# Three products of a two-block layer, each as seven chained products of halves

## The chip, the cores and the metric

One NeuronCore of one Trainium2 chip runs the whole program. The metric is the device time of one execution in microseconds. Three executions of the kernel before took 1607.38, 1607.43 and 1607.52 us.

## The reference, cut to what matters

The program computes two transformer-like blocks over 512 tokens of 1024 features in float32. The part that changes is the middle of the second block:

```
att  = forgetting_attention(q, k, v)            # 512 x 1024
mix  = gmlp_spatial_gating(z_u, z_v)            # 512 x 1024
ga, gb = sigmoid(gate columns)                  # 512 x 1024 each
h = x + (ga * (mix @ w_branch_a) + gb * (att @ w_branch_b)) @ w_out
h = h + ffn(rmsnorm(h))                         # starts with the product "up0"
```

Each of the three products is 512x1024 by 1024x1024.

## The kernel before, in words

**Precision.** A float32 product is made of three passes. Each operand is split into a high part (`fp32r`, by a ScalarE copy) and a low part (raw minus high, by a VectorE subtraction), and TensorE adds high x high, high x low and low x high in PSUM (`feature_k`).

**Weights.** All weights come as strips of 128x2048 floats (1 MB), 4 to a 1024x1024 matrix, through three slots (`w_raw`, which lies in the place of `w_lo`, and `w_hi`). The SyncE queue loads a strip as soon as the one three places back has been used; `hi(s)` on ScalarE and `lo(s)` on VectorE split it. Every engine works through an order of instructions that is written out by hand, and the engines meet in counting semaphores: `unit_done` (TensorE's half strips), `hi_split`, `strip_split`, `dve_evac` and others.

**The three products.** `stream("branch_b")`, `stream("branch_a")` and `stream("out2")` (lines 1277 to 1279) each run 8 output tiles of 128 features x 512 tokens, 24 matmuls of 512 columns each: 192 matmuls a product. The activations are `att_t` (split into `b_hi`, `b_lo` during the product before, `gate_a`), `u_t` (split into `a_hi`, `a_lo`) and `merged` (split tile by tile as it comes out). VectorE takes each tile out of PSUM as it multiplies by the gate, adds to `merged`, or adds to `x`. After `out2` tile m has been added to `x`, `high("ffn2")` and `low("ffn2")` split it for `up0`, the next product. GpSimd does nothing in this stretch. (Line 2116 adds a PSUM bank to `att_t` in SBUF.)

**Elsewhere** two kinds of products are already made of seven products of halves (`seven`, line 1172). There the sums of weight halves come from GpSimd's DMA queue: a transfer from DRAM that adds into a strip already in SBUF (`part_sums`, line 714). Each such transfer waits until the one before has landed.

Of the kernel before, what the change touches and what calls it, by code (L numbers as in the profile page):

```python
# [162 lines left out]
def build(nc, d, out):  # L163
    ctx = ExitStack()
    with ctx:
# [139 lines left out]

        up_pad = [sb(f"up_pad{j}", [P, CONV2 - 1 + T], at=work + 2048 + 520 * j) for j in range(4)]
# [104 lines left out]
        m_hi = sem("m_hi")  # L411
        m_lo = sem("m_lo")
# [10 lines left out]
        amix_hi = sem("amix_hi")  # L423
        amix_lo = sem("amix_lo")
# [32 lines left out]
        pool_out_ready, POOL_OUT0 = seg_done, SPARE0 + 32 * len(SEVEN)  # L457

# [73 lines left out]
        def _(sp_eng):  # L532
# [49 lines left out]

            for s in range(1, N_STRIPS):
# [6 lines left out]
                sp_eng.dma_start(w_raw[j].rearrange("p k n -> p (k n)"), d["strips"][STRIP_AT[s]]).then_inc(raw_loaded[j], 16)  # L590
# [4 lines left out]
                if s + 1 in MADE:  # L595
                    other_parts(SEVEN.index(next(name for name in SEVEN if FIRST[name] == s + 1)))
# [29 lines left out]
        def _(pool):  # L626
# [100 lines left out]
            attention("2b", "qk2b")  # L727
            for g in range(FF_SEVEN, len(SEVEN)):
# [9 lines left out]
        def _(pe):  # L738
# [630 lines left out]
        def _(act):  # L1369
# [416 lines left out]
            def sigmoids(phase, where):  # L1786
                for j in range(KT):
# [20 lines left out]
            for i in range(2, 4):
                hi(FIRST["branch_b"] + i + 2)
            for m in range(KT):  # L1810
                act.wait_ge(merged_ready, m + 1)
                if m == 0:

                    act.wait_ge(unit_done, 2 * FIRST["branch_a"])
                run(b_hi[:, m, :], merged[:, m * T:(m + 1) * T], ACT.Copy).then_inc(m_hi, 1)
                if m % 2 == 0:
                    hi(FIRST["branch_a"] + m // 2 + 2)
            for m in range(KT):
                act.wait_ge(dve_evac, EVAC0["out2"] + m + 1)
# [125 lines left out]
        def _(dve):  # L1945
# [959 lines left out]
```

## Time and profile before

| | us |
|---|---|
| median of three executions | 1607.43 |
| the profiled execution | 1607.59 |
| its span, first to last instruction | 1605.9 |
| TensorE busy in the span | 1587.6 (99%) |
| VectorE busy | 1078.5 (67%) |
| ScalarE busy | 710.6 (44%) |
| GpSimd busy | 181.5 (11%) |

Matmuls are pipelined, so their durations overlap: the pace is the distance between starts. An engine's row in order of time gives the start from the span's start, and the duration. "idle before <-" names what ended an idle time.

### The profile page before, as it was taken

To read this page: it belongs to the slowest core of one execution; us is meant where nothing else is said; L and a number is where in the kernel's file an instruction comes from. 1 tells how busy PE (TensorE), PEld (TensorE's weight loads), DVE (VectorE), ACT (ScalarE), POOL (GpSimd) and SP (SyncE) were. 2 spreads that over 40 slices of the span, in tenths; PEclk is the share of its full clock that TensorE was granted. 3 is DMA by queue.
4 is the path that set the end of the run, shared out by engine and by line. 5 is a ranking of instruction groups with operands and counts; after the bars stand their busy time and mean duration, and the time that the engine had idled before them with its cause. 6 is when DMAs were issued, how large, how long until landed. Compare 5 with 4: busy or idle time off the path is not lost.

```text
span 1605.9 us, 20446 instructions
## 1 busy us (share of the span) xinstructions
PE 1587.6 (99%) x8187; PEld 1305.8 (81%) x8187; DVE 1078.5 (67%) x1494; ACT 710.6 (44%) x1018; POOL 181.5 (11%) x263
## 2 busy tenths in 40 slices
PE   9999999999999999999999999999999999999998
PEld 7877777888888888878788887888888888888888
DVE  6756788669393865657744477445566876878857
ACT  6524575545252524415662156342334443443544
POOL 0001055000000000024500255000000000000000
PEclk9999999999999999999999999999999999999999
DMA  5233321264757522331022211322237347344221
GB/s 191 80 106 125 123 95 53 79 210 131 236 132 235 131 106 94 116 138 72 27 105 83 101 53 53 136 101 105 93 143 262 102 135 238 93 154 158 105 106 53
DMA packets 32894, 195.14 MB, mean 122 GB/s; under 512 B 4320, under 2 KB 6816, under 8 KB 11296
## 3 DMA queue, kind: packets, MB, share of 16 engines
q1 hardware_dynamic: 25056, 160.20, 27.0%
q0 software_dynamic: 2880, 20.97, 6.8%
q10 hardware_dynamic: 4864, 12.66, 2.2%
q8 instruction: 65, 1.06, 0.3%
q14 instruction: 29, 0.24, 0.0%
HBM read 187.50 MB, written 6.32 MB: 121 GB/s over the span
## 4 chain that ended last, share of the span: by engine, by line
PE 87%; DVE 7%; issue 2%; ACT 2%; POOL 1%; DMA 0%; DVEq 0%; ACTq 0%; POOLq 0%
PE bank L767 20%; PE bank L769 19%; PE bank L768 19%; PE bank L1189 3%; PE bank L1190 3%; PE bank L1191 3%; PE bank L815 3%; PE bank L817 3%; PE bank L816 3%; PE bank L1000 1%; PE bank L775 1%; PE bank L985 1%; DVE w_lo L2370 1%; PE bank L744 1%; DVE up_c L2668 1%
## 5 line engine op out<-in xcount | busy, mean ns | idle before, releaser
L767 PE MATMUL bank<-a_hi,w_hi 128*128 128x512 f32 x1160 | 456.8, 394 | 0.6 <-DVE x L2030 0.6
L769 PE MATMUL bank<-a_hi,w_lo 128*128 128x512 f32 x1160 | 452.0, 390 | 0.0
L768 PE MATMUL bank<-a_lo,w_hi 128*128 128x512 f32 x1160 | 451.6, 389 | 0.0
L1375 ACT ACTIVATE w_hi<-w_raw 128x2048 fp32r<-128x2048 f32 x95 | 181.3, 1908 | 184.5 <-DMA w_raw<-in_strips 182.7
L769 PEld LDWEIGHTS bank<-a_hi,w_lo 128*128 128x128 f32 x1160 | 217.8, 188 | 45.9
L767 PEld LDWEIGHTS bank<-a_hi,w_hi 128*128 128x128 f32 x1160 | 217.9, 188 | 45.3 <-issue 2.3
L768 PEld LDWEIGHTS bank<-a_lo,w_hi 128*128 128x128 f32 x1160 | 218.0, 188 | 43.0 <-issue 0.2
L1951 DVE TENSOR_TENSOR w_lo<-w_raw,w_hi 128x2048 fp32r<-128x2048 f32 x92 | 210.9, 2293 | 54.4 <-ACT w_hi L1375 54.3
L1189 PE MATMUL bank<-w_hi,t_hi 128*128 128x512 f32 x280 | 109.3, 390 | 0.1
L1191 PE MATMUL bank<-w_hi,t_lo 128*128 128x512 f32 x280 | 109.0, 389 | 0.0
L1190 PE MATMUL bank<-w_lo,t_hi 128*128 128x512 f32 x280 | 109.0, 389 | 0.0
L767 PE MATMUL bank<-b_hi,w_hi 128*128 128x512 f32 x240 | 93.6, 390 | 0.4 <-DVE b_lo L2684 0.4
L768 PE MATMUL bank<-b_lo,w_hi 128*128 128x512 f32 x240 | 93.4, 389 | 0.0
L769 PE MATMUL bank<-b_hi,w_lo 128*128 128x512 f32 x240 | 93.4, 389 | 0.0
L815 PE MATMUL bank<-w_hi,a_hi 128*128 128x512 f32 x224 | 90.8, 405 | 0.0
L714 POOL DMA_DIRECT2D a_part<-in_parts x20 | 17.4, 868 | 643.6 <-DMA a_part<-in_parts 431.9
L816 PE MATMUL bank<-w_lo,a_hi 128*128 128x512 f32 x224 | 87.4, 390 | 0.0
L817 PE MATMUL bank<-w_hi,a_lo 128*128 128x512 f32 x224 | 87.4, 390 | 0.0
L1845 ACT ACTIVATE up_c<-up_pad,conv_w 128x512 f32<-128x512 f32 x44 | 35.8, 816 | 115.1 <-DVE up_pad L2022 115.1
L2668 DVE SCALAR_TENSOR_TENSOR up_c<-up_pad,conv_w,up_c 128x512 f32<-128x512 f32 x88 | 65.8, 747 | 1.8 <-ACT up_c L1845 0.3
L2370 DVE TENSOR_TENSOR w_lo<-a_part,w_hi 128x2048 fp32r<-128x2048 f32 x25 | 57.1, 2285 | 10.7 <-ACT w_hi L1664 10.7
L2022 DVE TENSOR_TENSOR up_pad<-bank,rstd 128x512 f32<-128x512 f32 x44 | 30.3, 691 | 49.4 <-PE bank L769 49.4
(364 smaller groups left out, 2658.0 us busy)
## 6 DMA issues: line engine op xcount, KB each, us to landing
w_raw<-in_strips SPq DMA_DIRECT2D x107, 1024.0 KB, 4.8
a_part<-in_parts SPq DMA_DIRECT2D x25, 1024.0 KB, 7.4
a_part<-in_parts POOLq DMA_DIRECT2D x20, 1024.0 KB, 9.1
spare<-in_parts SPq DMA_DIRECT2D x5, 1024.0 KB, 15.0
spare<-in_strips SPq DMA_DIRECT2D x5, 1024.0 KB, 4.9
seg_in<-cum_kept ACTq DMA_DIRECT2D x16, 256.0 KB, 3.5
x_kept<-x ACTq DMA_DIRECT2D x2, 2048.0 KB, 9.2
x<-x_kept SPq DMA_DIRECT2D x2, 2048.0 KB, 9.9
```

The source lines that it names most:

```text
L767: mm(ps[:, :], w_hi[slot][:, k, cols], hi[:, k, :], start=(k == 0), stop=False)
L768: mm(ps[:, :], w_hi[slot][:, k, cols], lo[:, k, :], start=False, stop=False)
L769: return mm(ps[:, :], w_lo[slot][:, k, cols], hi[:, k, :], start=False, stop=(k == kt - 1))
L815: mm(bank[j][:, :], hi[:, q, tok], w_hi4[slot][:, k, :], start=(q == 0), stop=False)
L816: mm(bank[j][:, :], hi[:, q, tok], w_lo4[slot][:, k, :], start=False, stop=False)
L817: return mm(bank[j][:, :], lo[:, q, tok], w_hi4[slot][:, k, :], start=False, stop=(q == KT - 1))
L1189: mm(ps[:, :], hi[:, k, tok], w_hi4[slot][:, k, :], start=(first and k == 0), stop=False)
L1190: mm(ps[:, :], hi[:, k, tok], w_lo4[slot][:, k, :], start=False, stop=False)
L1191: last = mm(ps[:, :], lo[:, k, tok], w_hi4[slot][:, k, :], start=False, stop=(end and k == W4 - 1))
L1375: run(w_hi[j], w_raw[j], ACT.Copy).then_inc(hi_split, 1)
L1951: v.tensor_tensor(w_lo[j], w_raw[j], w_hi[j].bitcast(F32), ALU.subtract).then_inc(strip_split, 1)
L2668: v.scalar_tensor_tensor(up_c[q], up_pad[q][:, j:j + T], flat[:, at * (CONV2 + 1) + j:at * (CONV2 + 1) + j + 1], up_c[q], ALU.mult, ALU.ad ...
```

## The change

Each of the three products is cut into halves: the activation into four quadrants (256 tokens x 512 input features), the weight into four parts (512 x 512, one strip each), and the result is put together from seven products of a quadrant-sized activation by a part-sized weight, with sums and differences of quadrants and of parts as operands. One product is 4 output tiles x 4 input tiles x 3 passes = 48 matmuls of 256 columns; seven make 336.

- **Weights.** Of the seven weight operands two are parts as they are (products 2 and 6, loaded by SyncE into a slot). Two (products 0 and 4) are made in a buffer `fold_v`, and three (1, 3 and 5) in a buffer `fold_u`. In each buffer a first part is loaded by SyncE (`load_v`, `load_u`), and further parts are added by GpSimd's DMA (`add_part`), one add before products 1, 3, 4 and 5. An add changes the buffer in place, so it comes after the operand before it in that buffer has been split. All adds wait for the landing of the add before them, in the order of `FOLD_SUMS`. `fold_u` and `fold_v` of `branch_b` and `branch_a` are the same place; `out2` has its own, over `att_t`.
- **Low parts.** ScalarE still makes all high parts. VectorE makes the low parts of products 1, 2, 3, 5 and 6 (`low_strip`), GpSimd those of 0 and 4 (`low_v`, 128x2048).
- **Activations.** GpSimd makes four sums or differences of quadrants a product (`fold_sums`, 128x1024 each). Seven quadrant operands are split by ScalarE (`high_four`, `high_three`) and VectorE (`low_four`, `low_three`).
- **Results.** Products 0 and 2 are chained in banks 4 and 5, products 1 and 3 in 6 and 7, products 4 and 6 in 2 and 3; product 5 goes to 6 and 7. ScalarE copies the first link of two chains out before the next is added (`keep_first`, `keep_second`), VectorE takes out the rest (`take_first`, `keep_sums`, `take`) and multiplies or adds quadrants; for `out2` it adds known parts to `x` ahead of time (`add_known`).
- **Reload of x** moves from the end of `gate_a` to `branch_a`'s product 6, since `fold_v` and `fold_u` lie in `x`.
- **Before up0** VectorE's order is: `take_21`, the low part of `up0`'s first strip, feature tiles 0 to 3 of the split for `up0`, `take_12`, the second strip, tiles 4 to 7.

The diff, cut, with 12 leading spaces taken off:

```diff
+FOLD = ["branch_b", "branch_a", "out2"]
+QUADS = [(0, 0), (1, 0), (0, 1), (1, 1)]
+FOLD_BANK = [4, 6, 4, 6, 2, 6, 2]
+FOLD_QUAD = [0, 1, 2, 0, 1, 3, 2]
+FOLD_DIRECT = {2: (1, 0), 6: (1, 1)}
+V_STEPS, U_STEPS = [0, 4], [1, 3, 5]
+FOLD_ADD = {1: (1, 1), 3: (0, 0), 4: (0, 1), 5: (1, 0)}
+FOLD_SUMS = [(0, 1), (0, 4), (0, 3), (0, 5), (1, 1), (1, 4), (1, 3), (2, 1), (1, 5), (2, 4), (2, 3), (2, 5)]
+PHASES += [(name, 7) for name in FOLD]
...
+def load_v(f):
+    if f == 1:
+        sp_eng.wait_ge(pool_split, pool_count(0, 4))
+    sp_eng.dma_start(flat(fold_v[f]), fold_part(f, (0, 0))).then_inc(v_loaded, 16)
+def load_u(f):
+    if f == 1:
+        sp_eng.wait_ge(strip_split, FIRST[FOLD[0]] + 6)
+    sp_eng.dma_start(flat(fold_u[f]), fold_part(f, (0, 1))).then_inc(u_loaded, 16)
...
-    if s == FIRST["gate_a"] + 3:
+    if s == FIRST["gate_a"] + 2:
         sp_eng.wait_ge(pv_done, 2 * 3 * HEADS8)
+        load_v(0)
+        load_u(0)
+    if s == FIRST["branch_b"] + 2:
+        load_v(1)
+    if s == FIRST["branch_b"] + 6:
+        load_u(1)
+    if s == FIRST["branch_a"] + 2:
+        sp_eng.wait_ge(fold_step, FOLD_STEP0 + 5)
+        load_v(2)
+        load_u(2)
+    if s == FIRST["branch_a"] + 6:
+        sp_eng.wait_ge(strip_split, FIRST["branch_a"] + 6)
+        sp_eng.wait_ge(pool_split, pool_count(1, 4))
         sp_eng.dma_start(x, x_kept).then_inc(x_loaded[0], 16)
...
+def add_part(f, i):
+    if i == 1:
+        pool.wait_ge(u_loaded, U_LOADED0 + 16 * (f + 1))
+    elif i == 4:
+        pool.wait_ge(pool_split, pool_count(f, 0))
+    else:
+        pool.wait_ge(strip_split, FIRST[FOLD[f]] + i - 1)
+    landed, count = fold_count(f, i)
+    pool.wait_ge(landed, count - 16)
+    pool.dma_start(flat(fold_raw(f, i)), fold_part(f, FOLD_ADD[i]), accum_op=ALU.add).then_inc(summed, 16)
+def low_v(f, i):
+    s = FIRST[FOLD[f]] + i
+    pool.wait_ge(hi_split, s)
+    pool.tensor_tensor(w_lo[s % W_SLOTS], fold_v[f], w_hi[s % W_SLOTS].bitcast(F32), ALU.subtract).then_inc(pool_split, 1)
+def fold_sums(f, n):
+    src, at = fold_src[f], FOLD_SUM0 + 4 * f
+    a11, a12, a21, a22 = (quad(src, *q) for q in ((0, 0), (0, 1), (1, 0), (1, 1)))
+    if n == 0:
...
+        ins = pool.tensor_tensor(quad(fold_three[f], 1, 0), a11, a21, ALU.subtract)
+    elif n == 1:
+        pool.wait_ge(fold_sum, at + 1)
+        ins = pool.tensor_tensor(a21, a21, a22, ALU.subtract)
...
+    elif n == 2:
+        pool.wait_ge(fold_sum, at + 2)
+        pool.wait_ge(four_lo, 4 * f + 1)
+        ins = pool.tensor_tensor(a11, a21, a11, ALU.subtract)
+    else:
+        pool.wait_ge(fold_sum, at + 3)
+        pool.wait_ge(four_lo, 4 * f + 3)
+        ins = pool.tensor_tensor(a12, a12, a11, ALU.add)
+    ins.then_inc(fold_sum, 1)
+fold_sums(0, 0)
+add_part(0, 1)
+fold_sums(0, 1)
+fold_sums(0, 2)
+low_v(0, 0)
+add_part(0, 4)
+fold_sums(0, 3)
+add_part(0, 3)
+fold_sums(1, 0)
+fold_sums(1, 1)
+add_part(0, 5)
+low_v(0, 4)
+fold_sums(1, 2)
+fold_sums(1, 3)
+add_part(1, 1)
+low_v(1, 0)
+add_part(1, 4)
+add_part(1, 3)
+add_part(2, 1)
+add_part(1, 5)
+low_v(1, 4)
+low_v(2, 0)
+add_part(2, 4)
+fold_sums(2, 0)
+fold_sums(2, 1)
+add_part(2, 3)
+fold_sums(2, 2)
+fold_sums(2, 3)
+add_part(2, 5)
+low_v(2, 4)
...
+def folded(f):
+    for i in range(7):
+        s = FIRST[FOLD[f]] + i
+        slot, (t, k0) = s % W_SLOTS, QUADS[FOLD_QUAD[i]]
+        hi, lo = quad(fold_hi[f], t, k0), quad(fold_lo[f], t, k0)
+        if i in V_STEPS:
+            pe.wait_ge(pool_split, pool_count(f, i))
+        else:
+            pe.wait_ge(strip_split, s + 1)
+        if i in (3, 4, 6):
+            pe.wait_ge(three_lo, 3 * f + (3, 4, 6).index(i) + 1)
+        else:
+            pe.wait_ge(four_lo, 4 * f + (0, 1, 2, 5).index(i) + 1)
+        for h in range(2):
+            fold_bank(f, i, h)
+            for e in range(2):
+                ps = bank[FOLD_BANK[i] + h][:, e * (T // 2):(e + 1) * (T // 2)]
+                cols = slice((2 * h + e) * P, (2 * h + e + 1) * P)
+                for k in range(W4):
+                    mm(ps, w_hi4[slot][:, k, cols], hi[:, k, :], start=(e == 0 and k == 0 and i in (0, 1, 4)), stop=False, skip_group_check=True)
+                    mm(ps, w_hi4[slot][:, k, cols], lo[:, k, :], start=False, stop=False, skip_group_check=True)
+                    last = mm(ps, w_lo4[slot][:, k, cols], hi[:, k, :], start=False, stop=(k == W4 - 1), skip_group_check=True)
+            last.then_inc(unit_done, 1)
...
+def high_three(f, n):
+    t, k = QUADS[n]
+    act.wait_ge(fold_sum, FOLD_SUM0 + 4 * f + (3, 2, 4)[n])
+    act.wait_ge(unit_done, 2 * (FIRST[FOLD[f]] + n) + 2)
+    run(quad(fold_hi[f], t, k), quad(fold_src[f], t, k), ACT.Copy).then_inc(three_hi, 1)
...
+def keep_first(f):
+    act.wait_ge(four_lo, 4 * f + 4)
+    act.wait_ge(fold_sum, FOLD_SUM0 + 4 * f + 2)
+    for h in range(2):
+        act.wait_ge(unit_done, 2 * FIRST[FOLD[f]] + h + 1)
+        run(quad(fold_src[f], 1, 1, h), halves(4 + h), ACT.Copy).then_inc(snapped, 1)
...
+def low_strip(f, i):
+    s = FIRST[FOLD[f]] + i
+    j = s % W_SLOTS
+    dve.wait_ge(hi_split, s)
+    v.tensor_tensor(w_lo[j], fold_raw(f, i), w_hi[j].bitcast(F32), ALU.subtract).then_inc(strip_split, 2 if i - 1 in V_STEPS else 1)
...
+def keep_sums(f):
+    src, e0 = fold_src[f], EVAC0[FOLD[f]]
+    for h in range(2):
+        product_ready(f, 3, h)
+        dve.wait_ge(snapped, SNAPPED0 + 4 * f + h + 1)
+        v.tensor_tensor(quad(src, 0, 0, h), halves(6 + h), quad(src, 1, 1, h), ALU.add).then_inc(dve_evac, 1)
+    for h in range(2):
+        dve.wait_ge(dve_evac, e0 + 2 + h + 1)
+        dve.wait_ge(snapped, SNAPPED0 + 4 * f + 2 + h + 1)
+        fold_do(v.tensor_tensor(fold_q[h], quad(src, 0, 0, h), fold_q[h], ALU.subtract))
+def take(f, i, j, step, at):
+    src, e0 = fold_src[f], EVAC0[FOLD[f]]
+    for h in range(2):
+        product_ready(f, step, h)
+        known = {(1, 1): quad(src, 0, 0, h), (1, 0): quad(src, 1, 1, h), (0, 1): fold_q[h]}[i, j]
+        if f == 2:
+            part = quad(x, i, j, h)
+            ins = v.tensor_tensor(part, part, halves(FOLD_BANK[step] + h), ALU.add)
+        else:
+            ins = v.tensor_tensor(quad(src, 1, 0, h), halves(FOLD_BANK[step] + h), known, ALU.add if (i, j) == (1, 0) else ALU.subtract)
+        ins.then_inc(dve_evac, 1)
+    if f == 2:
+        return
+    dve.wait_ge(dve_evac, e0 + at + 2)
+    new, gate, total = quad(src, 1, 0), quad(gate3, i, j), quad(merged3, i, j)
+    if f == 0:
+        fold_do(v.tensor_tensor(total, total, new, ALU.mult))
...
+low_four(1, 0)
+low_strip(0, 2)
+low_three(0, 0)
+low_four(1, 1)
+low_strip(0, 3)
+low_three(0, 1)
+take_first(0)
+low_four(1, 2)
+low_three(0, 2)
+keep_sums(0)
+low_strip(0, 5)
+low_four(1, 3)
+take_22(0)
+low_strip(0, 6)
+take_21(0)
+low_strip(1, 1)
+take_12(0)
+low_strip(1, 2)
+low_three(1, 0)
+low_strip(1, 3)
+low_three(1, 1)
+take_first(1)
+low_three(1, 2)
+low_four(2, 0)
+keep_sums(1)
+low_strip(1, 5)
+take_22(1)
+low_strip(1, 6)
+take_21(1)
+low_strip(2, 1)
+take_12(1)
+low_four(2, 1)
+low_four(2, 2)
+low_four(2, 3)
```

ScalarE's order for one product is: high of product 2's weight, `keep_first`, `high_three` 0, `high_four` 1 of the next, high of 3, `keep_second`, `high_three` 1, high of 4, and so on to the next product's strips 0 and 1; `high_strip(f, 1)` stands ahead of `high_strip(f, 2)`.

## Rows read from the trace of the kernel before

**Rows 1.** The page: busy time by engine; the chain that ended last.
```profile
PE 1587.6 (99%) x8187; PEld 1305.8 (81%) x8187; DVE 1078.5 (67%) x1494; ACT 710.6 (44%) x1018; POOL 181.5 (11%) x263
...
PE 87%; DVE 7%; issue 2%; ACT 2%; POOL 1%; DMA 0%; DVEq 0%; ACTq 0%; POOLq 0%
```

**Rows 2.** Stretches: busy PE, PEld, DVE, ACT, POOL; PEclk; DMA share; GB/s.
```profile
1057.00:1101.00 44.00, 44.00 (x196) 36.44 (x195) 19.04 (x20) 10.36 (x10) 0.00 (x0) 1.00 0.26 97
1101.00:1145.00 44.00, 44.00 (x196) 36.44 (x195) 25.21 (x28) 12.28 (x12) 0.00 (x0) 1.00 0.27 96
1145.00:1188.00 43.00, 43.00 (x192) 35.59 (x191) 24.17 (x28) 17.79 (x22) 0.00 (x0) 1.00 0.28 98
```

**Rows 3.** TensorE in time: start us, duration us; 575 matmuls between.
```profile
1052.45 0.39 PE L767 MATMUL bank<-b_hi,w_hi 128*128 128x512 f32 x1
...
1183.01 0.39 PE L767 MATMUL bank<-a_hi,w_hi 128*128 128x512 f32 x1
```

**Rows 4.** TensorE in time, last stage; 95 matmuls between.
```profile
1571.76 0.28 PE L1325 MATMUL bank<-a_hi,w_hi 128*128 128x256 f32 x1
...
1583.28 0.28 PE L1325 MATMUL bank<-a_hi,w_hi 128*128 128x256 f32 x1
```

**Rows 5.** Groups by form, VectorE, ScalarE: busy us, mean ns | idle before.
```profile
L1951 DVE TENSOR_TENSOR w_lo<-w_raw,w_hi 128x2048 fp32r<-128x2048 f32 x92 | 210.9, 2293 | 54.4 <-ACT w_hi L1375 54.3
...
L2392 DVE TENSOR_TENSOR t_lo<-t_raw,t_hi 128x1024 fp32r<-128x1024 f32 x25 | 30.4, 1216 | 0.0
...
L1986 DVE SCALAR_TENSOR_TENSOR a_lo<-x,gains,a_hi 128x512 fp32r<-128x512 f32 x32 | 23.9, 750 | 25.0 <-ACT a_hi L1396 25.0
...
L2626 DVE TENSOR_TENSOR merged<-merged,bank 128x512 f32<-128x512 f32 x8 | 5.5, 686 | 24.5 <-PE bank L769 24.5
...
L1375 ACT ACTIVATE w_hi<-w_raw 128x2048 fp32r<-128x2048 f32 x95 | 181.3, 1908 | 184.5 <-DMA w_raw<-in_strips 182.7 <-issue 1.7
...
L1676 ACT ACTIVATE t_hi<-t_raw 128x1024 fp32r<-128x1024 f32 x25 | 26.5, 1059 | 39.3 <-DVE t_raw L2386 39.3
...
L1899 ACT ACTIVATE ple_t<-bank 128x512 f32<-128x512 f32 x8 | 4.1, 604 | 4.0 <-PE bank L1302 4.0
```

**Rows 6.** Groups by form, GpSimd.
```profile
L734 POOL TENSOR_TENSOR out_t<-x,rstd 128x256 f32<-128x256 f32 x2 | 1.4, 723 | 188.3 <-ACT rstd L1935 188.3
...
L674 POOL TENSOR_SCALAR score<-score,row_inv 128x512 f32<-128x512 f32 x8 | 5.6, 695 | 8.8 <-DVE row_inv L2105 8.6
...
L2896 POOL MEMSET const-float32-1.0<- 128x1 f32 x1 | 0.1, 98 | 0.0
```

**Rows 7.** VectorE and GpSimd in time, at two places.
```profile
710.11 2.28 DVE L1951 TENSOR_TENSOR w_lo<-w_raw,w_hi 128x2048 fp32r<-128x2048 f32 x1
...
710.28 2.58 POOL L667 TENSOR_SCALAR q_blk<-qk 64x512 fp32r<-64x512 f32 x1 [48.33 <-DVE qk L2022]
...
909.47 2.69 DVE L1951 TENSOR_TENSOR w_lo<-w_raw,w_hi 128x2048 fp32r<-128x2048 f32 x1
...
909.09 3.55 POOL L667 TENSOR_SCALAR k_blk<-qk 64x512 fp32r<-64x512 f32 x2
```

**Rows 8.** Line 2116: duration ns min/median/max.
```profile
L2116 DVE TENSOR_TENSOR att_t<-att_t,bank x16: 678/686/692, 754.6 to 1010.0; 64x512 f32<-64x512 f32 x16
```

**Rows 9.** DMA issues (KB, median us to landing); line 714; GpSimd in time.
```profile
w_raw<-in_strips SPq DMA_DIRECT2D x107, 1024.0 KB, 4.8
...
a_part<-in_parts SPq DMA_DIRECT2D x25, 1024.0 KB, 7.4
...
a_part<-in_parts POOLq DMA_DIRECT2D x20, 1024.0 KB, 9.1
...
DMA to landing us min/median/max: 7.6/9.1/13.1
...
1222.26 0.87 POOL L714 DMA_DIRECT2D a_part<-in_parts  x1 [8.18 <-DMA a_part<-in_parts]
```

**Rows 10.** TensorE in time, the first matmuls.
```profile
1.39 7.46 PE L1051 MATMUL bank<-b_lo 128*128 128x512 f32 x19 [1.39 <-POOL b_lo L628]
```

More of the change, by code:

```diff
@@ L1282, in _ @@
+            for f in range(len(FOLD)):
+                folded(f)
             stream("up0", feature_k, A, ready=wait_tiles(NORMS["ffn2"]["lo"]), after=lambda j: direct_sums("ffn2") if j == 0 else None)
@@ L1784, in _, with sigmoids @@
             attention("2b", "gate_b", None)
-            def sigmoids(phase, where):
-                for j in range(KT):
+            def sigmoids(phase, where, first, last):
+                for j in range(first, last):
                     act.wait_ge(dve_evac, EVAC0[phase] + j + 1)
@@ L1808, in _, with high_strip @@
[L1808 to L1819, printed above, removed]
+            def high_strip(f, i):
+                s = FIRST[FOLD[f]] + i
+                if i in FOLD_DIRECT:
+                    hi(s)
+                    return
+                act.wait_ge(*fold_count(f, i))
+                act.wait_ge(unit_done, 2 * (s - W_SLOTS) + 2)
+                run(w_hi[s % W_SLOTS], fold_raw(f, i), ACT.Copy).then_inc(hi_split, 1)
@@ new lines, in _ @@
+            high_strip(1, 6)
+            high_strip(2, 0)
+            high_strip(2, 1)
+            high_four(2, 1)
+            high_four(2, 2)
+            high_four(2, 3)
+            high_strip(2, 2)
+            keep_first(2)
+            high_three(2, 0)
+            high_strip(2, 3)
+            keep_second(2)
+            high_three(2, 1)
+            high_strip(2, 4)
+            high_three(2, 2)
+            high_strip(2, 5)
+            high_strip(2, 6)
+            hi(FIRST["up0"])
@@ new lines, in add_known @@
+            def add_known(i, j):
+                src = fold_src[2]
+                if (i, j) == (0, 1):
+                    for h in range(2):
+                        ins = v.tensor_tensor(quad(x, 0, 1, h), quad(x, 0, 1, h), fold_q[h], ALU.subtract)
+                elif (i, j) == (1, 1):
+                    ins = v.tensor_tensor(quad(x, 1, 1), quad(x, 1, 1), quad(src, 0, 0), ALU.subtract)
+                else:
+                    dve.wait_ge(snapped, SNAPPED0 + 8 + 2)
+                    ins = v.tensor_tensor(quad(x, 1, 0), quad(x, 1, 0), quad(src, 1, 1), ALU.add)
+                fold_do(ins)
@@ L2641, in _ @@
-            dve.wait_ge(x_loaded[0], 48)
-            for m in range(KT):
-                add_x("out2", m, m)
+                if 1 <= j <= 4:
+                    low_four(0, j - 1)
+                if j == 6:
+                    low_strip(0, 1)
+            low_four(1, 0)
[7 more added lines that the diff above has]
+            low_three(0, 2)
@@ L2644, in _ @@
+            take_22(2)
+            low_strip(2, 6)
+            take_21(2)
+            lo(FIRST["up0"])
+            for m in range(4):
                 low("ffn2", m, gains[:, 5, :], (a_hi, a_lo))
                 add_square("ffn2", m)
-                if m % 2:
-                    lo(FIRST["out2"] + m // 2 + 2)
+            take_12(2)
+            lo(FIRST["up0"] + 1)
+            for m in range(4, KT):
+                low("ffn2", m, gains[:, 5, :], (a_hi, a_lo))
+                add_square("ffn2", m)
@@ L2885 @@
         "strips": np.concatenate(strips),
[L2886 removed]
+        "parts": np.concatenate([by_half(w[j * D:(j + 1) * D]) for w, n in
+                                 ((ff2, FF_SEVEN), (down, 2), (g["w_branch_b_2"][0], 1), (g["w_branch_a_2"][0], 1), (g["w_out_2"][0], 1))
+                                 for j in range(n)]),
         "gains": np.stack([by_tile(v) for v in gains], axis=1),
```

245 lines of the change are left out of this document (184 added, 61 removed).

## The prediction

> **What bounds the kernel now.** I read the page first: TensorE is busy 99% of the span and makes up 87% of the chain that ended last [rows 1]. The stretches of the three products say the same: TensorE never idles, VectorE works 19 to 25 of 43 to 44 us, ScalarE 10 to 18, GpSimd nothing, DMA a quarter [rows 2]. From the first matmul of branch_b to the first of up0 pass 1183.01 - 1052.45 = 130.56 us for 576 matmuls, 0.2267 us each, with no gap [rows 3]. So only matmul time counts here, until something else becomes late.
>
> **What the change removes.** At equal speed per column, 7 products for 8 would save 130.56 / 8 = 16.3 us. But the new matmuls have 256 columns. The trace has such ones at the end: 96 starts in 1583.28 - 1571.76 = 11.52 us, 0.120 each [rows 4], where half of 0.2267 would be 0.113. A product is now 336 x 0.120 = 40.3 us (5.76 a step of 48) against 43.5. Gain: 3 x 3.2 = **9.6 us**, if TensorE is never kept waiting.
>
> **What it adds.** Prices per instruction [rows 5]: VectorE 2.29 (128x2048), 1.22 (1024), 0.69 (512 out of PSUM), 0.75 (a tile's low part); back to back each is some 0.08 less. ScalarE 1.90, 1.05, 0.60.
> VectorE, for branch_b: 5 weight low parts 11, 7 activation low parts 8, 10 tiles out of PSUM 6.5, two 512-wide differences 1.3, three multiplications 3.5: about 31 of 40 us; branch_a 36 with its four additions. ScalarE: 7 x 1.9 + 7 x 1.0 + 4 x 0.6 = 23; hidden.
> GpSimd: four 128x1024 sums, two 128x2048 low parts, four DMA issues of 0.87 [rows 9]. No such sizes are in the trace. The one two-input form is 128x256 at 0.723 [rows 6]. Upper bound, in proportion: 2.9 and 5.8. Lower bound, at the rate of the one-input form (0.695 for 512): 1.4 and 2.8. Less the 0.1 that an empty instruction takes, the row gives 2.6 and 5.1; some more may be fixed, so I take **2.35 and 4.5**. The Trainium skill (GPSIMD Engine Reference, "Elementwise — side-by-side cycle accounting") gives 4.497 for a two-input add of 2048 elements; no row shows it, and my sum would not change by it.
>
> **The two engines exclude each other.** VectorE's w_lo ran 710.11 to 712.39; a GpSimd instruction that began at 710.28 and usually takes 0.62 ended at 712.86. At 909.47 w_lo itself took 2.69 for 2.28, behind GpSimd [rows 7]. Sixteen VectorE instructions with one input in PSUM, in the same stages, never took over 0.692 [rows 8]. So I read: a VectorE instruction with two SBUF inputs and a GpSimd one run one after the other. The Trainium skill (SBUF — State Buffer, "SBUF: two separate sides") states it so, as an exclusive lock held for the whole instruction, against GpSimd instructions that read SBUF; the trace agrees by the 2.58 and 2.69. By this rule rival A below could not be; without it points 2, 5 and 6 would cost nothing.
> In branch_b that is 24 us of VectorE's two-SBUF work and 4 x 2.35 + 2 x 4.5 = 18.4 of GpSimd's, 42 us where TensorE needs 40.3, 47 in branch_a. Before, GpSimd's share was nothing.
>
> **The adds are in series.** Each add waits for the landing of the one before. An add lands 7.6 us after its issue at best, 9.1 in the median, 13.1 at worst; a plain load after 4.8, a pair at 7.4 [rows 9], so some 2.8 for a load that is in front. GpSimd's queue waits with it, as it did 8.18 us before its issue at 1222.26.
>
> **The walk.** I go through the written orders with these prices; times are from the span's start, and a stall is what TensorE waits. branch_b starts at 1052.5 as before: the first operands are made beside gate_a, where VectorE and GpSimd have room.
> 1. Step 2 needs a plain part whose load starts when gate_a ends, beside an add: landing 1060.7, +1.9 ScalarE, +2.3 VectorE: 1065.0 for 1064.0. Stall 1.0.
> 2. Step 5: its weight low part stands in VectorE's order behind the sums of step 3, two low parts and the differences. low_v of step 4 (4.5) and two fold_sums (2.35 each) come between them: 1084.1 + 2.3 = 1086.4 against 1082.3. Stall 4.2. (A 0.06 follows.) branch_a starts at 1098.0; the schedule of before has it at 1096.0, so the gain is spent.
> 3. branch_a, step 3. Only at 1086.4, with the low part of step 5, is fold_u free. Then in series: load 4.8 (1091.3), add for step 1 7.6 (1098.9), add for step 4 9.7 (a load is beside it: 1108.6), add for step 3 11.3 (out2's two first loads in front: 1119.9), ScalarE 1.9, VectorE 2.3: 1124.2. TensorE is there at 1115.3. Stall **8.9**.
> 4. Step 4 needs low_v on GpSimd, which stands behind two more issues, the second waiting for a landing at 1127.6; 0.9, ScalarE done by then, 4.5: 1133.4. Stall 3.4. Step 5: 0.3.
> 5. Step 6: VectorE takes out step 4 and multiplies (1141.9); GpSimd's low_v for out2 holds it until 1146.3; addition 1.2, low part 2.3: 1149.7. Stall 4.6.
> 6. out2 starts at 1155.5. Step 1 needs the second quadrant's low part, behind take_12 on VectorE, whose two SBUF instructions and this one each wait for a GpSimd sum: 1155.6 + 1.3 + 1.1 + 1.2 + 2.3 + 1.2 + 2.3 + 1.2 = 1166.2. Stall 4.9; step 2, 1.1. The rest of out2 keeps its pace, since its adds are ahead.
> 7. up0 begins on the tiles split before the end; tiles 4 to 7 come after take_12 (1.3), a strip's low part (2.3) and 1.3 a tile: stalls 1.0 and 0.4. Before, none [rows 3].
> Stalls 1.0 + 4.2 + 0.1 + 8.9 + 3.4 + 0.3 + 4.6 + 4.9 + 1.1 + 1.4 = 29.8. Less 9.6: **+20.1** (rounded terms). After that up0 goes on as before; I take nothing for its root of means, which comes some 2 us later against TensorE (0 to 2 us). The reload of x (issued 1139.5, needed 1174) is hidden.
> The profiled execution's span is 1605.9 and its time 1607.59; the median shown, 1607.43, is the span + 1.5. So 1605.9 + 20.1 + 1.5 = **1627.5 us**.
>
> **Bounds.** GpSimd at 1.4 and 2.8 gives about +11, at 2.9 and 5.8 about +28. Adds slower by 1.5 each (as the median has it) give some +10 more, in points 3 and 4. A fall of the granted clock from 2.4 to 1.2 GHz after a long stall isn't in the trace; its first 19 matmuls, up to 8.69, took 7.3 us where 19 x 0.227 are 4.3 [rows 10], so up to 3.0 a time, mostly beside other waits.
>
> **Rivals.**
> A. The two engines don't exclude each other in these forms (rows 7 show one-input GpSimd instructions only). Then points 2, 5 and 6 go, but the chain of point 3 remains: VectorE's low part ends about 1081.7, step 3 still stalls 8.9 from an earlier start, step 4 3.0. Total -9.6 + 0.9 + 8.9 + 3.0 + 0.7 + 0.2 + 1.4 = +5.5: 1612.9. For: no two-input form was seen in company. Against: both directions of waiting in rows 7.
> B. Faster: the serial chain of adds in point 3 is short enough. It decides there: with lows unblocked (1081.7) and each add landing like a plain load (4.8, which rows 9 never show: minimum 7.6), step 3 has its weight at 1081.7 + 4 x 4.8 + 4.2 = 1105.1, before 1110. Left are about 0.8 and 1.4: -9.6 + 2.2 = -7.4: 1600.0. It needs both conditions; with one alone the result is +5 to +8.
> C. More expensive: adds near 9.1 to 13.1 and GpSimd near its upper price, perhaps with the lower clock: +30: 1637.
> D. The stalls and the gain cancel by something between A and B: within 0.2% of before (3 us, about what a measurement of this kernel can tell).
>
> **Chances.** Forecast 0.52, A 0.16, B 0.09, C 0.20, D 0.03. Slower by over 0.2%: 0.52 + 0.16 + 0.20 = 0.88; within: 0.03; faster: 0.09. The range 1611 to 1639 takes in A and most of C; outside stay B, D and the end of C.
>
> **What would show it.** Right: the changed kernel's matmuls of 256 columns at 0.120; TensorE idle before them some 30 us between 1060 and 1210, the largest in branch_a before its product 3, released by VectorE's low part, this by ScalarE, this by the landing of an add; VectorE instructions of 1.22 and 2.29 grown by GpSimd's durations, those out of PSUM not; GpSimd idle on landings. Wrong: starts of up0's first matmul before 1183 (B); two-input rows of normal length beside a busy GpSimd (A); another pace than 0.120.

## The result, and the profile after

The changed kernel takes **1633.81 us** (1632.63 to 1634.19, four runs) where the kernel before takes 1607.41 (1606.43 to 1607.52) beside it: ratio **1.0164**, 95% interval 1.0147 to 1.0182. That is 26.4 us slower; forecast were 20.1 (1627.5, range 1611 to 1639).

The page of the changed kernel, against [rows 1]: TensorE is busy for the same 1588 us although its three products have an eighth fewer columns. In the chain that ended last its share falls from 87% to 79%, VectorE's grows from 7% to 10% and DMA's from 0% to 4%.

```profile
PE 1587.7 (97%) x8619; PEld 1325.9 (81%) x8619; DVE 1138.6 (70%) x1512; ACT 739.8 (45%) x1036; POOL 254.5 (16%) x293
...
PE 79%; DVE 10%; DMA 4%; issue 3%; ACT 3%; POOL 1%; DVEq 0%; ACTq 0%; POOLq 0%
```

The stretches of the three products, columns as in [rows 2]. TensorE works 42 of 49, 48 of 63 and 41 of 45 us; the granted clock (PEclk) averages 0.86 in `branch_a`; the DMA engines are some two to three times as busy as before (0.57, 0.71 and 0.52 for 0.26 to 0.28 [rows 2]).

```profile
1052.00:1101.00 49.00, 42.13 (x334) 41.62 (x333) 36.69 (x24) 21.84 (x20) 23.02 (x9) 0.97 0.57 151
1101.00:1164.00 63.00, 47.74 (x345) 46.93 (x344) 39.69 (x28) 21.98 (x17) 17.94 (x9) 0.86 0.71 184
1164.00:1209.00 45.00, 41.28 (x339) 40.69 (x338) 43.14 (x36) 22.85 (x24) 15.21 (x6) 1.00 0.52 141
```

What TensorE waited for between 1040 and 1215 (total, times, longest). The sum is 26.5 us, 29.8 were forecast, and the longest is the one at `branch_a` step 3:

```profile
PE bank L1478 <- DVE w_lo L2901: 21.1, 6, 8.8
PE bank L1478 <- issue: 3.1, 1, 3.1
PE bank L1478 <- POOL w_lo L832: 1.7, 1, 1.7
PE bank L929 <- DVE a_lo L2275: 0.6, 1, 0.6
```

The first matmul of `up0` starts at 1208.6 instead of 1183.0 [rows 3], 25.6 later. The balance: -9.6 for seven products at 0.120 a matmul, +25.8 of stalls up to there, +7.2 because the 48 matmuls behind four stalls took 7.33, 8.38, 7.23 and 7.35 us instead of 5.76, and some 2 around the stalls: the first matmul behind one takes 0.22 for 0.12, and the idle time is counted from the end of the last matmul, 0.28 after its start, where the pace is 0.12. Another 0.6 is the last wait above. The 3.1 put down to "issue" is the wait before `out2` step 1: VectorE's low part of the second quadrant ended at 1172.75, and TensorE went on at 1172.84.

**The chain of adds** (forecast point 3). SyncE's loads and GpSimd's queue, in time; in brackets, what GpSimd sat idle for:

```profile
1088.52 0.33 SPq L652 DMA_DIRECT2D fold_u<-in_parts  x1
...
1101.83 0.33 SPq L662 DMA_DIRECT2D w_raw<-in_parts  x1
1108.36 0.33 SPq L646 DMA_DIRECT2D fold_v<-in_parts  x1
```
```profile
1093.65 0.87 POOL L826 DMA_DIRECT2D fold_u<-in_parts  x1 [8.81 <-DMA fold_u<-in_parts]
1094.26 4.92 POOL L832 TENSOR_TENSOR w_lo<-fold_v,w_hi 128x2048 fp32r<-128x2048 f32 x1
1102.05 0.87 POOL L826 DMA_DIRECT2D fold_v<-in_parts  x1 [2.86 <-DMA fold_u<-in_parts]
1114.48 0.86 POOL L826 DMA_DIRECT2D fold_u<-in_parts  x1 [11.56 <-DMA fold_v<-in_parts]
1124.12 0.86 POOL L826 DMA_DIRECT2D fold_u<-in_parts  x1 [8.78 <-DMA fold_u<-in_parts]
```

The buffer is free at 1088.5 (forecast 1086.4). From there each issue follows the landing before: load 4.8, adds 7.9, 11.9 (with three plain loads beside it) and 9.1 us. From 1105 to 1119 the DMA engines are busy all the time (share 1.00, 287 GB/s). Then ScalarE (1.91) and VectorE, and TensorE starts step 3:

```profile
1125.55 2.29 DVE L2901 TENSOR_TENSOR w_lo<-fold_u,w_hi 128x2048 fp32r<-128x2048 f32 x1 [12.56 <-ACT w_hi L2001]
...
1148.64 5.49 DVE L2978 TENSOR_TENSOR merged<-merged,u_t 128x1024 f32<-128x1024 f32 x1
```
```profile
1127.90 0.58 PE L1478 MATMUL bank<-a_hi,w_hi 128*128 128x256 f32 x1 [8.82 <-DVE w_lo L2901]
1128.28 0.41 PE L1479 MATMUL bank<-a_lo,w_hi 128*128 128x256 f32 x1
1128.49 0.41 PE L1480 MATMUL bank<-a_hi,w_lo 128*128 128x256 f32 x1
...
1134.02 0.28 PE L1479 MATMUL bank<-a_lo,w_hi 128*128 128x256 f32 x1
1134.13 0.28 PE L1480 MATMUL bank<-a_hi,w_lo 128*128 128x256 f32 x1
...
1138.27 0.39 PE L1478 MATMUL bank<-a_hi,w_hi 128*128 128x256 f32 x1 [1.70 <-POOL w_lo L832]
```

After 8.82 us idle the starts are 0.213 apart until 1133.8, at a granted clock of 0.50, then 0.120: the lower of the two clocks (1.2 instead of 2.4 GHz), then the higher.

**The exclusion** (points 2, 4, 5). The row of 5.49 us above is an addition that takes 1.22 alone. Beside it GpSimd ran

```profile
1147.75 5.30 POOL L832 TENSOR_TENSOR w_lo<-fold_v,w_hi 128x2048 fp32r<-128x2048 f32 x1 [9.53 <-ACT w_hi L2001]
```

which ended at 1153.05; VectorE's addition ended 1.1 us after that, at 1154.1. GpSimd's own row is longer than the 4.6 us that it takes alone: it began while VectorE's instruction before, with two SBUF inputs too, ran until 1148.6, and 4.6 us behind that is 1153.2, near its end. The Trainium skill (SBUF — State Buffer, "SBUF: two separate sides") has it, for a VectorE instruction with two SBUF inputs against a GpSimd one that reads SBUF, as a lock that whoever starts first holds for the whole instruction; the trace agrees by these ends, in both directions.

### The profile page after: what moved, and what is told of

It reads as the page before. It is cut to its first block, busy times and chain, and to the rows that moved or that the text cites. A ratio compares the mean times of both kernels' runs of the same rounds, so it can differ in the third digit from the quotient of the medians.

```text
span 1632.5 us, 21442 instructions
## 1 busy us (share of the span) xinstructions
PE 1587.7 (97%) x8619; PEld 1325.9 (81%) x8619; DVE 1138.6 (70%) x1512; ACT 739.8 (45%) x1036; POOL 254.5 (16%) x293
## 3 DMA queue, kind: packets, MB, share of 16 engines
q1 hardware_dynamic: 25056, 160.20, 26.5%
## 4 chain that ended last, share of the span: by engine, by line
PE 79%; DVE 10%; DMA 4%; issue 3%; ACT 3%; POOL 1%; DVEq 0%; ACTq 0%; POOLq 0%
PE bank L929 17%; PE bank L931 16%; PE bank L930 16%; PE bank L1351 3%; PE bank L1352 3%; PE bank L1353 3%; PE bank L977 3%; PE bank L979 2%; PE bank L978 2%; DMA fold_u<-in_parts 2%; PE bank L1162 1%; PE bank L937 1%; PE bank L1147 1%; DVE w_lo L2901 1%; DMA fold_v<-in_parts 1%
## 5 line engine op out<-in xcount | busy, mean ns | idle before, releaser
L929 PE MATMUL bank<-a_hi,w_hi 128*128 128x512 f32 x1096 | 432.1, 394 | 1.2 <-DVE a_lo L2275 0.6
L931 PE MATMUL bank<-a_hi,w_lo 128*128 128x512 f32 x1096 | 427.1, 390 | 0.0
L930 PE MATMUL bank<-a_lo,w_hi 128*128 128x512 f32 x1096 | 426.7, 389 | 0.0
L929 PEld LDWEIGHTS bank<-a_hi,w_hi 128*128 128x128 f32 x1096 | 205.9, 188 | 44.0 <-issue 2.3
L931 PEld LDWEIGHTS bank<-a_hi,w_lo 128*128 128x128 f32 x1096 | 205.7, 188 | 43.5
L930 PEld LDWEIGHTS bank<-a_lo,w_hi 128*128 128x128 f32 x1096 | 206.0, 188 | 40.4 <-issue 0.2
L2240 DVE TENSOR_TENSOR w_lo<-w_raw,w_hi 128x2048 fp32r<-128x2048 f32 x80 | 184.4, 2306 | 55.5 <-ACT w_hi L1580 55.4
L1478 PE MATMUL bank<-b_hi,w_hi 128*128 128x256 f32 x224 | 64.5, 288 | 10.6 <-DVE w_lo L2901 7.5
L1480 PE MATMUL bank<-b_hi,w_lo 128*128 128x256 f32 x224 | 64.1, 286 | 0.0
L1479 PE MATMUL bank<-b_lo,w_hi 128*128 128x256 f32 x224 | 64.1, 286 | 0.0
```

The costliest lines, as they stand in the source:

```text
L929: mm(ps[:, :], w_hi[slot][:, k, cols], hi[:, k, :], start=(k == 0), stop=False)
L930: mm(ps[:, :], w_hi[slot][:, k, cols], lo[:, k, :], start=False, stop=False)
L931: return mm(ps[:, :], w_lo[slot][:, k, cols], hi[:, k, :], start=False, stop=(k == kt - 1))
L2240: v.tensor_tensor(w_lo[j], w_raw[j], w_hi[j].bitcast(F32), ALU.subtract).then_inc(strip_split, 1)
```

## The experiments

The steps of a product are called by its name and their number. Differences are taken from the changed kernel's 1633.8 and from the kernel before, measured beside each group (1606.8 to 1607.5).

### The width of the matmuls

```diff
-                mm(ps[:, :], w_hi[slot][:, k, cols], hi[:, k, :], ...)       # and two more
+                for c in range(2):
+                    t = slice(c * (T // 2), (c + 1) * (T // 2))
+                    mm(ps[:, t], w_hi[slot][:, k, cols], hi[:, k, t], ...)   # and two more
```

> The kernel before, with each 512-column matmul of branch_b, branch_a and out2 issued as two of 256 columns; nothing else. Theory (a 256-column matmul takes 0.120 us where half of a 512-column one takes 0.113): 1152 matmuls take 138.2 us instead of 130.6, the first matmul of up0 starts near 1190.7, the time is 1607.4 + 7.7 = 1615.1 (1614 to 1616.5). Rival (the 0.120 comes from the stalls, the order or the buffers of the changed kernel, not from the width): first matmul of up0 near 1183, time 1607.4 to 1609.

Measured 1614.99 (ratio 1.0050, 1.0035 to 1.0065). The first matmul of `branch_b`, and `up0`'s first:

```profile
1052.11 0.28 PE L776 MATMUL bank<-b_hi,w_hi 128*128 128x256 f32 x1
...
1190.35 0.40 PE L767 MATMUL bank<-a_hi,w_hi 128*128 128x512 f32 x1
```

138.24 us for 1152 matmuls, 0.120 each, no wait. So the price of the narrower matmuls, and with it the forecast's gain of 9.6 instead of 16.3, is right.

### GpSimd's arithmetic out, the adds out, both out

```diff
-                pool.tensor_tensor(w_lo[...], fold_v[f], w_hi[...], ALU.subtract)
+                pool.tensor_tensor(w_lo[...][:, :, 0:2], fold_v[f][:, :, 0:2], ...)   # fold_sums n > 0: 4 columns a row
```


> The changed kernel with GpSimd's arithmetic cut down: low_v and three of the four fold_sums of each product touch only 2 or 4 columns of each row (so their results are left out), order and waits as they are. Theory (GpSimd's durations and its exclusion of VectorE make the stalls of branch_b step 5, branch_a steps 4 to 6 and out2 step 1; the chain of adds alone makes the one of branch_a step 3): VectorE's 1.22 and 2.29 keep their length, step 3 of branch_a still stalls 7 to 9 us, the others together under 3, up0 starts near 1191, time 1617 (1613 to 1621). Rival (GpSimd's arithmetic is hidden, the adds are all): 1629 or more.


```diff
-                pool.dma_start(flat(fold_raw(f, i)), fold_part(...), accum_op=ALU.add).then_inc(summed, 16)
+                pool.dma_start(flat(fold_raw(f, i)), fold_part(...)).then_inc(summed, 16)
```


> The changed kernel with the twelve accumulating DMAs of the three products turned into plain loads of the same part into the same place (the sums of weight parts are left out), order and waits as they are. Theory (each link of the chain costs what an add costs more than a plain load): issue to landing falls from 7.9, 11.9, 9.1 us to about 5 to 7; the weight for branch_a step 3 is ready about 1116, before TensorE is there (1118.9): that stall of 8.8 and the lower clock behind it (2.6) go, some 3 us come back at steps 4 to 6, where GpSimd and VectorE are late: time 1625 (1621 to 1629). Rival (the landings are set by waiting in the queue, not by the add): 1631 or more.

> The two cuts together: plain loads for the accumulating DMAs, and GpSimd's low_v and three of four fold_sums on a few columns. Theory (the two causes are all of the stalls, what remains is the seven-for-eight gain at 0.120 a matmul, 9.6 us, less the load of branch_b step 2 of 1 to 3 us and the start of up0 of 1): 1602 (1599 to 1606), faster than the kernel before. Rival (TensorE's clock, the waits for PSUM banks or VectorE's own work keep it back): 1610 or more.

Measured 1624.26 (1.0103), 1619.20 (1.0077) and 1605.44 (0.9992, interval 0.9982 to 1.0001). TensorE's waits, for the first, the second and both:

```profile
PE bank L1480 <- DVE w_lo L2903: 17.2, 4, 8.8
PE bank L1480 <- issue: 1.4, 1, 1.4
...
```
```profile
PE bank L1478 <- DVE w_lo L2901: 7.7, 2, 4.1
PE bank L1478 <- issue: 3.1, 1, 3.1
PE bank L1478 <- POOL w_lo L832: 1.8, 1, 1.8
...
```
```profile
PE bank L1480 <- DVE w_lo L2903: 2.3, 1, 2.3
PE bank L1480 <- issue: 1.4, 1, 1.4
PE bank L931 <- DVE a_lo L2277: 0.7, 1, 0.7
```

The three kernels leave out sums, so their results are not the layer's; only their times count. The two causes together explain the loss: without both, 28.4 us are back where 26.4 had been lost, and the time can't be told from that of before. Taking out GpSimd's arithmetic brought less than expected (9.5 us, not 17, and outside the range that I gave): step 3 of `branch_a` still stalls 8.8, as expected, but `branch_b` step 5 and `branch_a` step 5 stall 2.3 and 4.1 although GpSimd's arithmetic is nearly gone. There an add is late too: the adds for these two steps landed 10.5 and 8.9 us after their issue, and with plain loads as well the first stall is gone and the second 2.3. Taking out the adds brought more (14.6, not 9, also outside its range). The stall at `branch_b` step 5 stays in either: it is the later of two chains, and the walk had named only one.

What an add costs beyond a load is in the DMA queues from 1040 to 1170 (packets, MB, share of the 16 engines' time), the changed kernel first, then with plain loads:

```profile
q0 software_dynamic: 1320, 9.63, 40.3%
q1 hardware_dynamic: 1440, 11.53, 23.3%
```
```profile
q1 hardware_dynamic: 1440, 11.53, 23.3%
q0 software_dynamic: 1440, 10.49, 21.8%
```

GpSimd's queue takes 4.2% a MB with the adds and 2.1% without, as much as SyncE's (2.0%). Issue to landing goes from a median of 8.0 to 5.1 us.

### TensorE kept at work in its waits

```diff
+                    for _ in range({(0, 5): 52, (1, 3): 130, (1, 5): 26, (1, 6): 40}.get((f, i), 0)):
+                        mm(bank[0][:, 0:P], ones_r, ones_r, start=True, stop=True)
```


> The changed kernel, with TensorE kept at work in its four waits that end in slower matmuls: 52, 130, 26 and 40 matmuls of ones into a bank that is free, ahead of the waits of branch_b step 5 and branch_a steps 3, 5 and 6. The 48 matmuls behind these waits should then take 5.76 us instead of 7.33, 8.38, 7.23 and 7.35, if the granted clock stays up. Theory (most of these 7.3 us is absorbed: what TensorE gains, it waits longer at the next step, because the chain of adds and GpSimd's low parts don't depend on it; only what lies behind the last product of branch_a is really on the path): 1.6 to 3 us faster than the changed kernel, 1631.5 (1630 to 1633). Rival (the lower clock adds up step by step): 1626.5.

Measured 1638.19 (1.0192): slower. The filling outlasted the waits, since one of its 128-column matmuls took 0.1118 us, nearly as much as one of 256 columns. So it says nothing of the clock; it gave the price for the next.

> e5_clock again with fewer filling matmuls, since each took 0.1118 us and not the 0.065 that I had counted with, so that the filling outlasted the waits: 30, 76, 14 and 22 in place of 52, 130, 26 and 40 (3.4, 8.5, 1.6 and 2.5 us, a little under the waits of 3.6, 8.8, 1.9 and 2.8). The steps behind should take 5.8 us again. Theory (absorbed: only what lies behind the last product of branch_a is on the path): 1 to 3 us faster than the changed kernel, 1632 (1630.5 to 1633). Rival (the lower clock adds up): 1626.5 to 1628.

Measured 1635.18 (1.0171; 1630.3 to 1638.8). The step behind the longest wait now runs at full pace, and the next wait is longer: 4.4 us before step 4 instead of 1.7.

```profile
1115.05 8.60 PE L1465 MATMUL bank<-ones_r 128*128 128x128 f32 x76
1123.49 0.33 PE L1480 MATMUL bank<-a_hi,w_hi 128*128 128x256 f32 x1
1123.65 0.28 PE L1481 MATMUL bank<-a_lo,w_hi 128*128 128x256 f32 x1
...
1133.88 0.39 PE L1480 MATMUL bank<-a_hi,w_hi 128*128 128x256 f32 x1 [4.43 <-POOL w_lo L832]
```

From the first matmul of step 3 to the first of step 4 pass 10.39 us; in the changed kernel, with the lower clock, 10.37. From the first of step 6 to the first of `out2` step 1 it is 16.28 and 16.33. At these two places the wait takes all that the clock gave back. The profile is that of the fastest of the four runs; `up0` starts 3.9 us earlier in it than in the changed kernel, but 3.4 of them are there already at `branch_b` step 2, ahead of any filling, where the wait is 0.4 instead of 3.3. The filling before step 3 also lasted 0.4 us longer than VectorE's low part. So the rival, some 7 us of gain, is refuted. Whether it is the 1 to 3 of the theory or none can't be told from runs 8.5 us apart.

### Adds that don't wait for each other

```diff
+            if i == 4:
+                return v_summed, 16 * (f + 1)
...
             add_part(1, 3)
-            add_part(2, 1)
             add_part(1, 5)
             low_v(1, 4)
+            add_part(2, 1)
             low_v(2, 0)
```

(`FOLD_SUMS`, which counts the landings, is shortened to the adds into `fold_u`.)

> The changed kernel, with a semaphore of their own for the adds into fold_v, so that an add into fold_u no longer waits until an add into fold_v has landed, and with out2's first add issued behind low_v of branch_a step 4 instead of ahead of branch_a's last add. The result is complete. Theory (the 8.8 us stall is the four landings in series; the add for step 3 then needs only the first add and the low part of step 1, is issued about 1106 and lands about 1115 to 1117): stall before branch_a step 3 of 1 to 3 us, step 5 no longer behind an add of out2, time 1622 (1619 to 1626). Rival (the adds then share the DMA engines with each other and with out2's two loads, and land after 12 us or more): stall 5 or more, 1628 or more.

Measured **1622.83** (1.0097): 11 us faster than the changed kernel, with the same work. GpSimd issues the add for step 3 at 1104.7, 9.8 us earlier, when VectorE has freed the buffer:

```profile
1097.81 0.87 POOL L829 DMA_DIRECT2D fold_v<-in_parts  x1 [0.30 <-POOL w_lo L835]
1104.66 0.86 POOL L829 DMA_DIRECT2D fold_u<-in_parts  x1 [5.98 <-DVE w_lo L2904]
```

The add for step 3 lands 11.7 us after its issue, nearly as late as the rival had it, but the wait before step 3 is 1.9 us instead of 8.8; one of 1.1 before step 2 is new. Two things were changed at once, the semaphore and the place of `out2`'s first add; how much of the 11 us each is worth isn't shown.

### GpSimd's arithmetic moved to VectorE

```diff
-                pool.tensor_tensor(w_lo[s % W_SLOTS], fold_v[f], ...).then_inc(pool_split, 1)
+                v.tensor_tensor(w_lo[s % W_SLOTS], fold_v[f], ...).then_inc(pool_split, 1)
```


> The changed kernel with the six low_v (128x2048) on VectorE instead of GpSimd, each in the order between the low parts around it; GpSimd keeps the fold_sums and the adds. The result is complete. Theory (one low_v costs VectorE's two-SBUF-input work 4.6 us by exclusion where VectorE itself needs 2.3): stalls of branch_a steps 4 to 6 shrink by 2 to 4 us, the chain of adds remains as in e2_narrow, time 1628 (1624 to 1631). Rival (VectorE, with 41 to 46 us of work for 40.3 of TensorE, becomes the bound): 1634 or more.

> e6_own_count and e7_low_on_vector together, the result is complete. Theory (stalls are the later of the two chains, so that shortening one alone leaves most of them, and both together give more than the sum): 1614 (1609 to 1619), so still slower than the kernel before. Rival (the effects only add up, or VectorE is the bound): 1620 or more.

> e8_low_and_count with the fold_sums on VectorE too, so that GpSimd does no arithmetic in the three products and only issues the adds; out2's first activation sum and the low part that follows it stand ahead of the last tiles of branch_a in VectorE's order. The result is complete. Theory (exclusion costs more than the work itself: a sum is 2.4 us on GpSimd and 1.22 on VectorE, and the stall of 6.2 before out2 step 1 is a sum on GpSimd that waits for a DMA issue ahead of it): no VectorE instruction above 2.3 us, stall before out2 step 1 of 2 to 3, time 1614 (1611 to 1617). Rival (VectorE, now with 41 us in branch_b and 46 in branch_a for 40.3 of TensorE, is the bound): stalls in every step behind VectorE's low parts, 1620 or more.

Measured 1626.94 (1.0127), 1618.83 (1.0072) and 1617.80 (1.0062, 1.0045 to 1.0079). Work moved onto the busier engine made the kernel faster by 6.9 us, with the own count by 15.0: a low part is 2.3 us on VectorE, and 4.6 to 5.3 on GpSimd in which VectorE may be held. But the two changes together (15.0) give less than their sum (6.9 + 11.0 = 17.9), where I had expected more, although the time lies in the expected range. The largest wait is then 6.2 us before `out2` step 1, where GpSimd's sums hold VectorE; the last kernel was to remove it. With all of it on VectorE none of its rows is stretched (mean 2290 and 2286 ns for the low parts of `fold_u` and `fold_v`):

```profile
L2854 DVE TENSOR_TENSOR w_lo<-fold_u,w_hi 128x2048 fp32r<-128x2048 f32 x8 | 18.3, 2290 | 6.9 <-ACT w_hi L1954 6.6
...
L2860 DVE TENSOR_TENSOR w_lo<-fold_v,w_hi 128x2048 fp32r<-128x2048 f32 x5 | 11.4, 2286 | 0.0
```

and yet the last move brought only 1.0, within what these runs can tell from nothing, where 1614 had been expected. The wait before `out2` step 1 is gone, but 1.2 and 3.5 us stand before steps 0 and 2. The largest stall (4.4 us) is now before `branch_a` step 2; `branch_b` step 2 waits 2.3. The plain parts of these two steps, `branch_b` first, landed so long after their issue:

```profile
DMA to landing us min/median/max: 9.4/9.4/9.4
...
DMA to landing us min/median/max: 11.5/11.5/11.5
```

### The transfers kept apart

```diff
+                if (f, i) in ((0, 3), (1, 4)):
+                    direct = FIRST[FOLD[f]] + 2
+                    pool.wait_ge(raw_loaded[direct % W_SLOTS], raw_count(direct))
...
                     sp_eng.wait_ge(fold_step, FOLD_STEP0 + 5)
+                    sp_eng.wait_ge(strip_split, FIRST["branch_a"] + 4)
```


> e10_all_vector, with the transfers kept out of each other's way: the add for branch_b step 3 and the add into fold_v for branch_a step 4 are issued only when the plain part for step 2 of their product has landed, and out2's two first loads wait for the low part of branch_a step 3. Same transfers, same sums, the result is complete. Theory (the stalls of 2.3 and 4.4 us before step 2 of branch_b and branch_a come from a plain load of 1 MB that lands after 9.4 and 11.5 us because an add is beside it, where alone it takes 4.8): both stalls and the lower clock behind them (1.6 each) go, the load lands within 7 us, some 3 us come back because the delayed adds are later: time 1610 (1607.5 to 1614), still not below the kernel before. Rival (those loads are late for another reason, or the delayed adds cost as much as they free): 1616 or more.

Measured 1626.25 (1.0114): 8.5 us slower than the kernel that it starts from, so the rival of 1616 or more is right: the delayed adds cost more than they free. Half of the theory held: TensorE no longer waits before either step 2, and the same two parts landed in

```profile
DMA to landing us min/median/max: 6.1/6.1/6.1
...
DMA to landing us min/median/max: 4.7/4.7/4.7
```

But each delayed transfer met the next. These are GpSimd's issues around the delayed adds; the one at 1124.7 lands 13.9 us later, beside the two loads that had been put off:

```profile
1107.03 0.85 POOL L833 DMA_DIRECT2D fold_v<-in_parts  x1 [13.79 <-issue]
1107.57 1.21 POOL L833 DMA_DIRECT2D fold_u<-in_parts  x1
1124.68 0.86 POOL L833 DMA_DIRECT2D fold_u<-in_parts  x1 [15.91 <-DVE w_lo L2858]
```

`branch_b` step 5 and `branch_a` steps 3 and 5 wait 4.5, 5.4 and 5.4 us. A collision moved is not a collision removed.

### Exclusion by itself

```diff
+            for j in range(8):
+                pool.wait_ge(unit_done, 2 * FIRST["branch_a"] + j + 1)
+                for n in range(2):
...
+                    pool.tensor_tensor(scratch, steps01, steps01, ALU.subtract).then_inc(company, 1)
```


> The kernel before, with two subtractions of 128x512 on GpSimd per tile of branch_a (16 in all, on constants, into space that nobody reads): some 1.2 us each, 20 of 43.5 us. Theory (GpSimd and a VectorE instruction with two SBUF inputs exclude each other, but VectorE's 25 us and GpSimd's 20 have room in two-per-tile pace while TensorE is at work 43.5 us): VectorE's w_lo of 2.29 and its 0.7 instructions without PSUM input grow by up to 1.2 where they meet one, those out of PSUM stay at 0.68, TensorE never waits, time as before, 1607 (1606 to 1608.5). Rival (no exclusion of whole instructions): no VectorE instruction longer. Rival (exclusion reaches TensorE here too): 1610 or more.

Measured 1607.18 (1.000, 0.9991 to 1.0009). VectorE and GpSimd in `branch_a`:

```profile
L2644 DVE TENSOR_TENSOR merged<-merged,gate_t 128x512 f32<-128x512 f32 x8 | 7.2, 895 | 0.3
...
L2642 DVE TENSOR_TENSOR gate_t<-gate_t,bank 128x512 f32<-128x512 f32 x8 | 5.5, 684 | 12.2 <-PE bank L777 12.2
```
```profile
1112.32 4.43 POOL L735 TENSOR_TENSOR scratch<-steps 128x512 f32<-128x512 f32 x2 [0.67 <-PE bank L777]
1117.76 1.04 POOL L735 TENSOR_TENSOR scratch<-steps 128x512 f32<-128x512 f32 x1 [1.01 <-PE bank L777]
```

One takes 1.04 us alone; two that begin 0.2 us behind a low part of VectorE (2.28) take 4.43, about the sum. The additions with two SBUF inputs grow from 692 ns on average (the kernel before) to 895, those with a bank as input stay at 684. And TensorE doesn't notice: with VectorE's rows at 27 and GpSimd's at 21 of 44 us, waits for each other included, exclusion costs no time here.

## Why the prediction was right

- **Pace, 9.6 us of gain:** right, shown by the halved matmuls.
- **Points 1 to 7:** forecast 1.0, 4.3, 8.9, 3.7, 4.6, 6.0 and 1.4 us of stall; measured 3.3, 3.6, 8.8, 3.6, 2.8, 3.7 and 0.6. Each place was right, the sizes less so: point 4 fits only as a sum (3.4 and 0.3 were forecast, 1.7 and 1.9 measured), and the errors have both signs, so that part of the agreement of the total is luck. Point 1 was too small: the plain load took 10.4 us beside an add, where I had counted 8.2, and it is the add that does it (beside a plain transfer the same load took 7.1, and this stall is gone).
- **Point 2 had half of its cause.** I put it down to GpSimd's sums in VectorE's way. Cutting these leaves 2.3 us, cutting the adds leaves 3.6.
- **Point 3:** the place, the chain of releasers and the stall were as forecast. The links were 4.8, 7.9, 11.9 and 9.1 us for 4.8, 7.6, 9.7 and 11.3: `out2`'s two loads met the second add and not the third, so that the sums agree (33.7 and 33.4) is partly luck. The order was what could be mended: 11 us by one semaphore and one exchange.
- **GpSimd's prices:** forecast 2.35 and 4.5; alone they take 2.4 and 4.6.
- **The 6.3 us missed:** in the sum, stalls were 3.3 too large, and matmuls at the lower clock (7.2), which I had named and left out as lying mostly beside other waits, and the ends and starts around each stall (some 2) were absent. Filling the waits bears the reason out at two of the four places, where 4.2 of the 7.2 us turned into longer waits: there the lower clock hid stalls and cost nothing. By this estimate the stalls at full clock would have been near 31 us, not 26.5. What the other 3.0 us cost stays open.
- **Rival A** (no exclusion, 1612.9) was refuted by the rows; its price was too good as well, since with GpSimd's arithmetic nearly gone the time is 1624.3. **Rival B** (both conditions, 1600.0) had its conditions made by hand and gave 1605.4: `branch_a` step 5 still waits 2.3 for VectorE, `out2` step 1 waits 1.4, `up0` 0.7, and 1.6 us go at the lower clock.

No version beat the kernel before. The best complete one is at 1617.8; the one without adds and most of GpSimd's arithmetic, at 1605.4, is not to be told from it.

## What to carry to other kernels

A saving in matmuls is a loan on the other engines: price the operands it needs (here 12 adding transfers and 18 GpSimd instructions for 16.3 us of matmuls, of which the narrower ones keep only 9.6), and check each buffer's chain from "free" to "split" against TensorE's arrival, not the engines' busy shares. When two chains are nearly equally late, name both, because cutting one shows little. A semaphore shared by independent transfers, and work put on an idle engine that locks out a busy one, are the first things to mend.

## What the runs showed of the hardware

- An adding transfer of 1 MB takes twice the DMA engines' time of a plain one (4.2 against 2.1% a MB in the same stretch). Three plain loads issued 1.0 to 2.3 us behind an add landed after 9.4, 10.4 and 11.5 us, one behind a plain transfer after 7.1, the median one of the kernel before after 4.8 [rows 9]. A load issued 0.2 us ahead of an add landed after 5.7, and the add after 11.9.
- Matmuls of 128, 256 and 512 columns start 0.112, 0.120 and 0.227 us apart with a weight load each. From 256 to 128 columns a matmul gets only 0.008 us shorter. The Trainium skill (TensorE: Matmul & The Clock Gate, "LDWEIGHTS (loading the stationary operand)") gives 128 columns / 1.2 for a weight load, 107 ns; the 112 measured lies 5 above that. That the weight load sets this pace is likely but not shown: the rows of the loads overlap and last 0.19 us each.
- The granted clock fell after stalls of 1.9 to 8.8 us in four places of the changed kernel and not after 3.3 and 3.1 us in two others (before `branch_b` step 2 and `out2` step 1). With plain loads for the adds the wait before `out2` step 1 was 3.1 us again, and this time the step behind it took 7.3 us instead of 5.8. So the length of one stall alone doesn't tell.
